# Up units of a two-layer diffusion step: the fourth weight sum as a GpSimd tensor add in place of an accumulating DMA

## The reference, cut to what matters

```python
h2 = _rmsnorm(x, norm2_g[l]) * (1 + sc2) + sh2
a, b = jnp.split(_dwconv3(h2 @ w_up[l], ffn_conv_w[l]), 2, axis=-1)   # D_FF = 2816
x = x + g2 * ((jax.nn.silu(a) * b) @ w_down[l])
```

## Time and profile before

| what | value |
|---|---|
| median of 3 runs | 1589.41 us (1584.88 to 1589.67) |
| the profiled execution, its own time | 1589.34 us |
| its span, first to last instruction | 1587.5 us |
| mean granted share of TensorE's clock | 0.991 |
| busy: PE, PEld | 1563.4 us, 1458.6 us |
| busy: DVE, ACT, POOL | 1028.2 us, 724.0 us, 165.5 us |
| accumulating DMAs | 160, 256 KB each |

### The profile page before, as it was taken

One profiled execution on the slowest core, in us unless ns is written; L12 is line 12 of the kernel. 1 busy time (PEld: TensorE's weight loads), 2 busy tenths in 40 slices (PEclk: granted clock), 3 DMA queues, 4 the chain that ended last, 5 costly groups with the idle time before them and its releaser, 6 DMA issues. The chain is left out here.

```text
span 1587.5 us, 26411 instructions
## 1 busy us (share of the span) xinstructions
PE 1563.4 (98%) x10573; PEld 1458.6 (92%) x10573; DVE 1028.2 (65%) x1661; ACT 724.0 (46%) x1218; POOL 165.5 (10%) x197
## 2 busy tenths in 40 slices
PE   8999999999999999999999999999999999999998
PEld 6678889988999999999987788899899999999998
DVE  6762666737775765757777547685687667476673
ACT  5434454326552643525444344542565355263452
POOL 1000000003211202112000000000221120120210
PEclk9999999999999999999999999999999999999999
DMA  9554010465756957769553621033377585694862
GB/s 360 201 191 152 28 54 28 160 210 156 179 146 158 215 137 170 184 153 209 155 175 109 207 71 54 27 107 108 93 161 178 142 196 150 153 207 137 193 156 84
DMA packets 284511, 236.13 MB, mean 149 GB/s; under 512 B 10698, under 2 KB 254724, under 8 KB 284388
## 3 DMA queue, kind: packets, MB, share of 16 engines
q1 hardware_dynamic: 260064, 189.89, 38.1%
q0 software_dynamic: 24080, 44.45, 16.2%
q10 hardware_dynamic: 244, 0.09, 0.0%
HBM read 188.78 MB, written 3.67 MB: 121 GB/s over the span
## 5 line engine op out<-in xcount | busy, mean ns | idle before, releaser
L1633 ACT ACTIVATE w_hi<-raw_all 128x1024 fp32r<-128x1024 f32 x120 | 126.2, 1056 | 234.1 <-DMA raw_all<-raw_all 113.4
L2230 DVE TENSOR_TENSOR w_lo<-raw_all,w_hi 128x1024 fp32r<-128x1024 f32 x120 | 146.6, 1222 | 115.3 <-ACT w_hi L1633 114.9
L1240 PE MATMUL ps<-gg,w_hi 128*128 128x322 f32 x704 | 218.5, 310 | 0.0
L1242 PE MATMUL ps<-gg,w_lo 128*128 128x322 f32 x704 | 218.2, 310 | 0.0
L1241 PE MATMUL ps<-gg,w_hi 128*128 128x322 f32 x704 | 218.1, 310 | 0.0
L666 POOL DMA_DIRECT2D raw_all<-raw_all x160 | 136.4, 868 | 620.6 <-DMA raw_all<-in_w_up_dram 493.9
L1185 PE MATMUL ps<-hc_lo,w_hi 128*128 128x322 f32 x640 | 199.5, 312 | 0.0
L1183 PE MATMUL ps<-hc_hi,w_hi 128*128 128x322 f32 x640 | 198.9, 311 | 0.0
L1187 PE MATMUL ps<-hc_hi,w_lo 128*128 128x322 f32 x640 | 198.6, 310 | 0.0
L1183 PE MATMUL ps<-ht_hi,w_hi 128*128 128x322 f32 x480 | 150.1, 313 | 5.6 <-ACT s L1651 5.2
L2125 DVE SCALAR_TENSOR_TENSOR x<-ps,modv,x 128x128 f32<-128x128 f32 (+2 forms) x240 | 90.4, 434 | 93.6 <-PE ps L1242 54.5
(11 more groups left out here) (235 smaller groups left out, 3488.9 us busy)
## 6 DMA issues: line engine op xcount, KB each, us to landing
raw_all<-in_w_up_dram SPq DMA_DIRECT2D x280, 256.0 KB, 3.8
raw_all<-raw_all POOLq DMA_DIRECT2D x160, 256.0 KB, 4.0
raw_all<-in_w_in_dram SPq DMA_DIRECT2D x48, 512.0 KB, 5.1
raw_all<-in_w_mod_dram SPq DMA_DIRECT2D x48, 512.0 KB, 4.3
raw_all<-in_w_down_dram SPq DMA_DIRECT2D x16, 768.0 KB, 4.5
raw_all<-in_w_down_dram SPq DMA_DIRECT2D x16, 640.0 KB, 4.1
mod_q<-in_w_mod_dram SPq DMA_DIRECT2D x8, 1024.0 KB, 9.1
raw_all<-in_w_out_dram SPq DMA_DIRECT2D x16, 512.0 KB, 4.3
```

What stands on the lines that cost most here:

```text
L1240: mm(out, wh[:, k, :], gh, start=k == 0, stop=False)
L1242: ins = mm(out, wl[:, k, :], gh, start=False, stop=k == kf - 1)
L1633: A(whi_b[:, 2 * i:2 * (i + 1), :], src, ACT.Copy).then_inc(up_hi[i], 1)
L2230: V.tensor_tensor(wlo_b[:, pair, :], raw_b[:, pair, :] if i else first_pair(g), whi_b[:, pair, :].bitcast(F32), ALU.subtract).then_inc(up_ ...
```

## The change

GpSimd computes sum 5 with a tensor add of its own, 128x512 floats from SBUF to SBUF, in the place in its stream where the accumulating DMA was issued. The semaphore `sum5_ready` goes up by one when the add is done; the three places that waited for the DMA's landing wait for it. All other waits, and the order of all streams, are unchanged.

```diff
-        sum_full = {b: sem("sum_full%d" % b) for b in (1, 2, 4, 5)}
+        sum_full = {b: sem("sum_full%d" % b) for b in (1, 2, 4)}
+        sum5_ready = sem("sum5_ready")
...
                     if i:
                         sp.wait_ge(up_lo[1], n)
-                        sp.wait_ge(sum_full[5], 16 * n)
+                        sp.wait_ge(sum5_ready, n)
                     block(2, 0, 0, g)
...
                         sp.wait_ge(up_lo[1], su(l, last) + 1)
-                        for b in (2, 4, 5):
+                        for b in (2, 4):
                             sp.wait_ge(sum_full[b], summed(l, last))
+                        sp.wait_ge(sum5_ready, su(l, last) + 1)
...
                     add_block(4, 0, 4)
                     pool.wait_ge(sum_full[2], summed(l, g))
                     pool.wait_ge(blk_full[5], loaded(l, g, 5))
-                    add_block(5, 2, 5)
+                    b2, b5 = (raw_f[:, b * BLK:(b + 1) * BLK] for b in (2, 5))
+                    nc.gpsimd.tensor_tensor(b5, b5, b2, ALU.add).then_inc(sum5_ready, 1)
...
                     else:
                         act.wait_ge(sum_full[4], summed(l, g))
-                        act.wait_ge(sum_full[5], summed(l, g))
+                        act.wait_ge(sum5_ready, su(l, g) + 1)
                     A(whi_b[:, 2 * i:2 * (i + 1), :], src, ACT.Copy).then_inc(up_hi[i], 1)
```

## The result

The changed kernel took 1579.54 us (median of 5 runs, 1577.34 to 1580.46) against 1589.41 us for the kernel before (5 runs, 1584.88 to 1590.66): a ratio of **0.9934**, 95% interval 0.9915 to 0.9953. A second measurement, on another occasion, gave 0.9936 (0.9917 to 0.9955). That is 10 us faster, 7.5 to 13.5 by the interval. The forecast was 6.3 us faster, with a range from 1581.0 to 1588.0: the direction and the cause were right, the size was not.

The account below looks back on a forecast made before the run. PE was taken as the bound, idle in the MLP only while waiting for ACT's copy `s`. 1589.34 - 7.0 (stalls) + 0.7 (left and new ones) = 1583.0 us, range 1581.0 to 1588.0.

Parts of the forecast that it names:

- PE is the bound and waits for `s` because sum 5 is the last to arrive: MLP up units: PE, busy 98%, waits for ACT's copy `s`, since sum 5 lands last, by 1.3 us at the mean.
- A stall costs 0.16 us more than PE's idle time: PE's waits for `s`: twelve stalls taken as 7.0 us, lower bound 5.2 and upper 8.8, all to be removed.
- Plus 0.7 us for what is left and what is new: Added back to the time: stalls that remain, and new ones of a tenth each behind the port, 0.7 us.
- Nothing outside the MLP: The sum's only terms were 7.0 us of stalls in the MLP and 0.7 us back; none lay elsewhere.
- The add takes 1.2 us, 2.4 at worst: GpSimd's 128x512 add for sum 5: 1.2 us with start-up, 2.4 us if it must wait for DVE.
- Sum 4 is next late: Ahead of pair 2's split: with sum 5 early, sum 4's landing decides, and ACT starts 2.0 us sooner in the unit shown.
- ACT's wait for landings: Sign of being right: ACT's wait at L1633 for DMA landings gets shorter by 25 to 50 us.
- SyncE's wait at L588: Sign of being right: SyncE's wait for sum 5 ahead of loading block 2, 31.6 us over 25 waits, gone or small.
- The next sum 1 has room: GpSimd's queue behind the add: the next unit's first sum, held 0.35 to 1.55 us more, still has several microseconds.
- The rival `c22`: The add holds off DVE's `gate_lo`, so `c22` exceeds 1.04 us of slack and PE's seventh product waits: 1594 to 1601, chance 0.09.

Follow-up runs that it names:

- sum 4 alone: The kernel before, with sum 4 (not sum 5) added by GpSimd and sum 5 still an accumulating DMA: 1604.34 us, ratio 1.0085.

## Why the prediction was wrong in size and right in cause

- *PE is the bound and waits for `s` because sum 5 is the last to arrive.* Right: sum 5 was last in all 30 units, by 1.9 us at the mean (I had 1.3 from SyncE's waits). Holding sum 5 back brought the stalls back in full.
- *A stall costs 0.16 us more than PE's idle time, the twelve together 7.0 us, with 8.8 as the upper bound.* **This term failed.** They cost 8.8 us in that very execution, by the length of its MLP against one without waits. The step into a stall was read rightly (1.84 us more than the usual 0.15 in the earlier trace rows), but the step out of it was left out: the next matmul follows after some 0.25 us, not 0.15, in all twelve stalls. Together that is 1.95 us, which is what the weight loads' row has for this stall:

```profile
1210.52 0.31 PE L1185 MATMUL ps<-ht_lo,w_hi 128*128 128x322 f32 x1
...
1210.26 0.19 PEld L1183 LDWEIGHTS ps<-ht_hi,w_hi 128*128 128x128 f32 x1 [1.95 <-ACT s L1651]
```

  So the row that was taken as the upper bound was the cost itself. Besides, this execution was the mildest of three (8.8 us, against 10.4 and 9.1), and the row bounds only the execution that it comes from. Over three profiles each the MLP lost 8.7 us, where the forecast had 7.0 - 0.7 = 6.3.
- *Plus 0.7 us for what is left and what is new.* Right in size: 1.6, 1.1 and 0 us in the weight loads' rows, 0 with both sums on GpSimd. With 8.8 in place of 7.0 the sum gives 1581.2 us, just inside the range, and with the mean of the three rows, 9.4, it gives 1580.6, just below it; 1579.54 was measured. The prediction had the baseline right but leaned on the run of 1584.88 as a sign that the gain could be smaller; it was the lowest of five, and of 63 later runs of that kernel (1584.21 to 1597.67) only one took less.
- *Nothing outside the MLP.* The pair of profiles has 1.6 us there. The rest of the span is 708.9 to 710.0 us in three profiles before and 705.3 to 708.2 in three after; among the other runs it is 706.1 to 709.9. All streams are alike there, and the three profiles before happen to have more time at half the granted clock (23.9 to 29.6 us) than those after (18.5 to 25.0), while over all runs the mean granted share is 0.993 for both kernels. I take it for scatter, of which the interval of the ratio (7.5 to 13.5 us) has room for all; that it is no more than that was not shown, and these last 1 to 2 us stay open.
- *The add takes 1.2 us, 2.4 at worst.* 1.29 alone, 1.51 at the mean, 2.58 at worst: right. *Sum 4 is next late*: right, in 25 to 28 of 30 units, by 0.9 to 1.2 us. ACT's wait for landings fell further than the 25 to 50 us named, from 113.4 to 26.2, but 57.5 us of that is now a wait for PE (16.2 before, 73.7 after), so it gained PE nothing. SyncE's wait at L588 is gone, as named.
- *The next sum 1 has room.* Right for an add. It is less than I thought: one more DMA ahead of it ate the whole gain.
- *The rival `c22`.* It didn't come, with 40 adds or with 80 GpSimd operations; with sum 4 alone the weight loads waited for it twice, 0.4 us in all. Full blocking by the lock is what the Trainium skill's page "SBUF — State Buffer" has in "SBUF: two separate sides". The timelines of the run with sum 4 alone agree in the main, in both directions: the add got in only at `c11`, and DVE's 0.82 us became 1.53, 0.71 more where the add had 0.84 still to run. Mean DVE times rose from 0.82 to 1.03 us for `gate_lo` and from 1.222 to 1.243 for the pair splits. So the mean delay is 0.2 us, and the longest of `gate_lo` in that profile, 1.05 us, is about the 1.04 us of slack: the blocking is there and costs PE nothing in the changed kernel.

The range should have reached below 1579: stalls of 8.8 us as the middle and not the end, and room for an execution that differs from the one profiled, when the three quoted runs spread over 4.8 us.

## What to carry to other kernels

When a chain waits for several results, find which arrives last and by how much, and shorten that one: a small engine add of 1.5 us in place of a 4.4 us DMA won 0.65% here, the same exchange on the neighbouring sum lost 0.85%. Before moving work onto GpSimd, see what DVE does at that moment: beside operations with one PSUM input it is nearly free, in a run of operations with two SBUF inputs it waits for the run's end, and what stands behind it in the queue waits too. Take the cost of stalls from the weight loads' waits rather than from PE's, and from several executions, not from one.

## What was unexpected of the hardware

A 128x512 add on GpSimd took 1.29 us alone and up to 3.97 us amid DVE operations with two SBUF inputs; it got in when DVE ran one with an input from PSUM. Accumulating DMAs of 256 KB landed after 4.0 us at the median, but single ones after 7.4 us (with another issued 0.6 us ahead in GpSimd's queue) and 7.6 us (in the changed kernel, without the extra DMA). A matmul that had been stalled was followed by the next after 0.25 us, in all twelve stalls of the kernel before, where 0.15 is usual. A GpSimd memset of 128x512 took 0.55 us. All kernels are identical up to the first MLP, and yet its first matmul started anywhere between 369.6 and 374.6 us.
